# ScalarE does a unit's four exponentials before its predecessor's four copies, in the attention of a hybrid diffusion trunk

## The reference

```
q, k, v = split((x * (1 + scale) + shift) @ w_in)
# 8 neighbourhood heads of 64: a latent query sees a clamped 8 x 16 window of the grid
# and the 128 context keys, with a bias by relative position
p = softmax(concat(q k_window / 8 + bias, q k_ctx / 8))
o = p_window v_window + p_ctx v_ctx
# 4 differential heads of 2 maps of 64: all latent and all context keys
a = softmax(q1 k1 / 8) - lam * softmax(q2 k2 / 8)
o = a v
# context queries: only context keys, no window
```

## Time and profile before

| | |
|---|---|
| median of three runs | 2249.7 us (2246.43 to 2251.04) |
| the profiled execution | 2250.41 us, span 2248.6 us |
| attention block in it | from 344.3 us to 503.3 us |
| busy over the span | PE 2048.4 us, DVE 1595.3 us, ACT 1246.2 us |
| granted TensorE clock | 0.949 over the span, 0.85 in the attention block |

### The profile page before, as it was taken

How to read it: one execution, slowest core, us unless ns; L and a number is a source line. 1 busy time by engine, 2 the same in 40 slices (tenths; PEclk the granted TensorE clock), 3 DMA queues, 4 the chain that set the end, 5 groups by cost and what they waited for, 6 DMA issues and landing times.

```text
span 2248.6 us, 24769 instructions
## 1 busy us (share of the span) xinstructions
PE 2048.4 (91%) x9780; PEld 1396.3 (62%) x9780; DVE 1595.3 (71%) x1444; ACT 1246.2 (55%) x1279; POOL 271.4 (12%) x109
## 2 busy tenths in 40 slices
PE   7899996877844999999999999999999999999992
PEld 7866665656742666666666666666666666666661
DVE  0111014554226999989999899898998989989885
ACT  0100004540033777777777777777777777777771
POOL 0001000000002020211202112021120210202100
PEclk9999997988856999999999999999999999999996
DMA  9821110002224999999999999999999999999982
GB/s 364 334 83 57 43 58 23 6 11 86 75 81 157 405 363 390 375 363 403 361 391 375 364 399 368 385 378 364 398 363 391 379 363 398 362 390 379 370 343 99
DMA packets 96994, 634.98 MB, mean 282 GB/s; under 512 B 11088, under 2 KB 16592, under 8 KB 23920
## 3 DMA queue, kind: packets, MB, share of 16 engines
q1 hardware_dynamic: 91632, 615.65, 70.2%
q0 software_dynamic: 5248, 17.75, 3.0%
HBM read 618.36 MB, written 14.20 MB: 281 GB/s over the span
## 4 chain that ended last, share of the span: by engine, by line
issue 47%; POOL 10%; DMA 7%; PE 4%; DVE 2%; ACT 0%; SPq 0%; POOLq 0%; DVEq 0%; ACTq 0%
DMA place<-x_rows,place 6%; POOL place L941 3%; POOL place L948 2%; POOL acc_rows L952 2%; POOL place L939 2%; PE ps L999 1%; PE ps L994 1%; PE ps L995 1%; PE ps L1011 0%; PE ps L1016 0%; PE ps L1012 0%; DVE place L1085 0%; DVE place L169 0%; DMA place<-mod_rows 0%; DVE place L1110 0%
## 5 line engine op out<-in xcount | busy, mean ns | idle before, releaser
L1085 DVE TENSOR_TENSOR place<-ring,place 128x2048 fp32r<-128x2048 f32 x528 | 1283.1, 2435 | 110.3 <-ACT place L1046 102.6
L1046 ACT ACTIVATE place<-ring 128x2048 fp32r<-128x2048 f32 x528 | 1012.6, 1918 | 372.9 <-PE ps L999 232.6
L994 PE MATMUL ps<-place 128*80 128x512 f32 x1408 | 560.5, 398 | 2.4 <-ACT place L1046 2.4
L995 PE MATMUL ps<-place 128*80 128x512 f32 x1408 | 552.7, 393 | 0.0
L999 PE MATMUL ps<-place 128*80 128x512 f32 x1408 | 380.7, 392 | 0.8 <-DVE place L1085 0.8
L999 PEld LDWEIGHTS ps<-place 128*80 128x80 f32 x1408 | 208.2, 148 | 116.8 <-DVE place L1085 1.9
L1011 PE MATMUL ps<-place 128*80 128x512 f32 x704 | 280.0, 398 | 0.0
L1012 PE MATMUL ps<-place 128*80 128x512 f32 x704 | 276.3, 392 | 0.0
L994 PEld LDWEIGHTS ps<-place 128*80 128x80 f32 x1408 | 208.4, 148 | 107.3 <-issue 3.3
L995 PEld LDWEIGHTS ps<-place 128*80 128x80 f32 x1408 | 209.1, 149 | 104.1 <-issue 0.5
L948 POOL TENSOR_TENSOR place<-place 80x1024 f32<-80x1024 f32 x16 | 55.0, 3439 | 1139.3 <-ACT place L1037 1139.3
(11 more groups left out here) (138 smaller groups left out, 1530.9 us busy)
## 6 DMA issues: line engine op xcount, KB each, us to landing
ring<-in_w_exp SPq DMA_DIRECT2D x528, 1024.0 KB, 6.7
ring<-in_w_ada SPq DMA_DIRECT2D x24, 1024.0 KB, 8.9
place<-in_w_in SPq DMA_DIRECT2D x12, 1024.0 KB, 7.9
ring<-in_w_out SPq DMA_DIRECT2D x4, 1024.0 KB, 10.6
place<-in_xT SPq DMA_DIRECT2D x1, 2560.0 KB, 23.0
place<-in_x SPq DMA_DIRECT2D x1, 2560.0 KB, 9.1
x_rows<-place POOLq DMA_DIRECT2D x5, 512.0 KB, 3.6
acc_rows<-place POOLq DMA_DIRECT2D x5, 512.0 KB, 5.6
```

The lines of the kernel that those rows point to most:

```text
L994: eng.matmul(out, xH[:, e % 2, kk, :], w, start=(kk == 0), stop=False)
L995: eng.matmul(out, xL[:, e % 2, kk, :], w, start=False, stop=False)
L1046: eng.activation(wH[:, n % SPLITS, :], ring[:, (FIRST_EXPERT_CHUNK + n) % RING, :], ACT.Copy).then_inc(wh_done, 1)
L1085: eng.tensor_tensor(wL[:, n % SPLITS, :], ring[:, (FIRST_EXPERT_CHUNK + n) % RING, :], wH[:, n % SPLITS, :].bitcast(F32), ALU.subtract).th ...
```

## The change

Only ACT's list in the attention block changes. In iteration k its order was copy 0, copy 1, exp 0, exp 2, copy 2, exp 1, exp 3, copy 3, the copies being those of unit k-1 and the exponentials those of unit k. It becomes exp 0, exp 2, exp 1, exp 3, copy 0, copy 1, copy 2, copy 3.

```diff
                 for k in range(UNITS + 1):
-                    if k >= 1:
-                        copy_turned(k - 1, 0)
-                        copy_turned(k - 1, 1)
                     if k < UNITS:
                         exp(k, 0)
                         exp(k, 2)
-                    if k >= 1:
-                        copy_turned(k - 1, 2)
-                    if k < UNITS:
                         exp(k, 1)
                         exp(k, 3)
                     if k >= 1:
-                        copy_turned(k - 1, 3)
+                        for n in range(4):
+                            copy_turned(k - 1, n)
```

## The result

The changed kernel takes 2270.59 us (median of four runs, 2268.88 to 2271.87) against 2249.47 us of the kernel before beside it (2246.43 to 2251.04): a ratio of 1.0095, 95% interval 1.0078 to 1.0113, 21 us slower. The forecast was 2267 with a range of 2256 to 2272. The profiled execution took 2268.88 us.

The account below looks back on a forecast made before the run. The attention block was taken as bound by a loop between engines, its last wait the scores' for the exponentials. Order 8.3 us plus clock 8.9 us gave 17.2 us on the 2249.7 median: 2267, range 2256 to 2272.

Parts of the forecast that it names:

- The exponentials end 1.76 us earlier: ACT, high latent iteration: four exponentials run from their first maximum, leaving ACT free at 414.73 instead of 416.49.
- The scores follow the tail: PE: near products 0, 1 and turns 2, 3 follow copy 0, ahead of scores; high iteration 8.14 us against 7.67.
- Low iterations: Latent iterations with scores at 1.2 GHz: 9.62 us against 9.26, +0.36 each.
- Context iterations: Four attention iterations at the lower clock: scores about 0.3 us later each, the first losing more; 1.5 us in all.
- The end: Last iteration: weigh_all(18) waits for copy 3, which now comes after a late turn 3; 0.75 us.
- Sum of the order: Attention block at an unchanged share of low iterations: 1.5 + 8 x 0.48 + 6 x 0.36 + 0.75 = 8.3 us.
- The clock: Longer, emptier PE stretch before scores: thirteen of fifteen latent iterations low instead of seven, 6 x 1.48 = +8.9 us.
- Passed on whole: After the attention block all engines meet and its loads are long finished, so its whole loss reaches the kernel time.
- A: PE's work between copy 0 and scores binds, clock changes little: +8.3 us, up to three more low iterations, 2258 to 2262; chance 0.20.
- D: All latent iterations low, some losing in both the scores and the PE work before them: near 2272; chance 0.09.
- B: Clock stays high in all latent iterations: 8.3 - 10.4 = -2 us, 2248, no change that can be told; chance 0.06.
- C: Scores follow the exponentials, released 1.76 us earlier, in each of fifteen latent iterations: -26 us, 2223; chance 0.03.

Follow-up runs that it names:

- the filled kernels: Extra matmuls, results never read, in PE's idle time of the latent iterations: five added to the changed kernel, 2251.58 us; three added to the kernel before, 2239.33 us.
- the copies between the pairs: Against the changed kernel, ACT does copies 0 and 1 after exp 0 and exp 2, before exp 1 and exp 3: 2231.87 us, 0.9916.
- the near products late: Against the changed kernel, PE does near products 0 and 1 of a unit behind the next unit's scores: 2232.96 us, 0.9921.

## Why the prediction was right, step by step

- *The exponentials end 1.76 us earlier.* Right: copy 0 at S + 5.71.
- *The near product waits for copy 0, about 2.3 us.* Right: 2.29 us.
- *The scores follow the tail and no longer the exponentials; +0.48 us in a high iteration.* The mechanism is right, the size was 0.59, chiefly since the handover from turn 3 to the scores was put at 0.22 us and is 0.32. I read it from the pace of matmuls within a group.
- *Low iterations 9.62 us.* Near: the iteration from 418.57, whose scores are low, takes 9.77. But the 8.14 us of a high iteration never came in the changed kernel; its iterations are 9.04 to 9.82 us, with one of 11.46, since each has some low time.
- *Context iterations, 1.5 us.* Too small: the first part of the block grew by 2.5 us, of which 0.5 is the clock at k = 0 (2.4 between the filled kernels). The iteration k = 1 alone went from 3.96 to 4.87 us, 0.9; I had given the others 0.3 each, they took about 0.4 (0.7 the last, between the filled kernels).
- *The end, 0.75 us.* 0.85 between the filled kernels, 0.55 between the plain ones.
- *Sum of the order, 8.3 us.* It is the term that was mis-sized: 11.8 us at the higher clock. It is 7.7 for thirteen iterations at 0.59, 0.9 for k = 5 (9.91 against 8.97 us in the filled kernels, partly low in both), 2.4 for the context iterations and 0.85 for the end, where the prediction had 6.0 for the fourteen latent iterations, 1.5 and 0.75.
- *The clock, +8.9 us.* Measured 9.2, or 8.7 without the half microsecond at k = 0. It was counted as thirteen low iterations in place of seven; in fact every iteration has some low time, but often less than the 3.3 us of a low one before: 42.9 us against 20.9, 22 more, which at 3.3 us is six to seven. So the amount was right and its form, whole low iterations beside high ones, was not.
- *Passed on whole.* Right by the medians: block +21.0 us, medians +21.1. Outside the block single profiled executions differ by up to 5 us (2087.6 to 2092.9 over all kernels here), so a single time says less about a change in the block than the block's own stretch does.
- *The total.* 21 us where 17.2 was forecast; the median lies 1.4 us inside the upper end of the range.

Of the rivals, A (the tail binds, the clock changes little) had the mechanism and not the clock. D, the end of the range, had its premise come true, every iteration partly low; low on both sides at full length happened once, in the iteration from 369.46, which took 11.46 us at clock 0.65. B and C had nothing for them.

The prediction's larger estimate, 20 us with all fifteen iterations low, is nearer to the 21 measured than its own sum, but by luck: its clock term (11.8) was too large and its term for the order (8.3) too small. The Trainium skill's section on psum-queue depth-cycling (TensorE: Matmul & The Clock Gate), beside which it stood, says that short idles between groups of matmuls make the clock go to and fro and cost throughput. The trace agrees: filling them won 0.6% in the kernel before.

## What to carry to other kernels

An engine's longest wait is not yet a wait on the loop: before moving the waiting instruction, follow what its result releases, and what that engine has queued in front of the next turn of the loop. Place a copy out of PSUM so that what its consumer still has to do runs under other work of the copying engine, and does not make that engine wait for its producer either; here that is between exponentials, best after the first, neither before nor behind all of them. And where a loop leaves TensorE idle for a part of every iteration, read the granted clock of each iteration, since shortening the gap can pay twice, in time and in clock, and here even filling it paid.

## What the runs showed of the hardware that was not expected

- How little separates a clock that falls from one that does not. With PE idle 1.38 us before the scores, seven of fifteen latent iterations had a low stretch; with 0.99 us idle and nothing else changed but a copy's place, the clock was 1.00 over 94.67 us. This is one execution of that kernel: over the whole span its clock was 0.952, and 0.947 to 0.951 in its four others, so it may have fallen in them.
- One long idle can be enough. The order with the copies after exp 0 leaves PE idle 0.28 and 0.44 us an iteration, and yet one iteration took 8.65 us and the next, partly at the lower clock, 7.94:

```profile
394.48 4.52 POOL L303 TENSOR_TENSOR place<-place 128x2048 f32<-128x2048 f32 x1 [5.95 <-DMA place<-in_far]
...
396.91 2.77 DVE L629 SCALAR_TENSOR_TENSOR place<-place 128x640 f32<-128x640 f32 x1
...
402.55 0.88 PE L545 MATMUL ps<-place 128*128 128x64 f32 x6 [2.17 <-ACT place L586]
...
405.05 1.23 PE L498 MATMUL ps<-place 64*128 64x256 f32 x4 [0.16 <-ACT place L575]
```

DVE's last step of `combine` took 2.77 us where it takes 0.89 in the iteration before. POOL was at its one large addition of this stretch at the time; that POOL slows it is not tested, but the same step is long under the same addition with the copies between the pairs (1.83 us, then 1.73 us of idle PE and a fall of the clock) and with the near products late (2.38 us, 1.45 us idle and no fall).
- Extra work that nobody reads makes the kernel faster: five useless matmuls in each of fifteen iterations took the changed kernel from 1.0095 to 0.9997 of the kernel before, and three took the kernel before to 0.9944.
- The low time arranges itself with the loop. The changed kernel's iterations come in fours (9.50, 9.29, 9.77, 9.09 us, then 9.50, 9.27, 9.73, 9.12), those before in twos (7.67 and 9.3).
